# A mixture-of-experts kernel on one core: the last block of tokens merged on chip, and its output loads issued one scatter earlier

## What is computed

```python
# top-1 of 4 groups, then top-2 of 8 experts in it: 2 of 32 experts per token
combine = jnp.sum(one_hot(expert_idx, 32) * p_exp[..., None], axis=1)
for e in range(32):
    hid = silu(t @ w_gate[e]) * (t @ w_up[e])        # 1024 -> 256
    out = out + combine[:, e:e + 1] * (hid @ w_down[e])
x = x + out
y = x * rsqrt(mean(x * x) + 1e-6) * g_final
```

## Time and profile before

| what | value |
|---|---|
| time, median of 3 runs | 535.07 us (533.61 to 535.42) |
| the profiled execution, its own time | 534.76 us |
| its span | 532.9 us |
| granted TensorE clock, mean | 0.972 of full speed |
| PE busy in the span | 480.9 us (90%) |
| DVE busy | 237.9 us (45%) |
| ACT busy | 100.4 us (19%) |
| POOL busy | 201.0 us (38%) |
| DMA, mean over the span | 265 GB/s |

### The profile page before, as it was taken

How to read it: one execution, slowest core, us unless ns; L and a number is a source line. 1 busy time by engine, 2 the same in 40 slices (tenths; PEclk the granted TensorE clock), 3 DMA queues, 4 the chain that set the end, 5 groups by cost and what they waited for, 6 DMA issues and landing times.

```text
span 532.9 us, 8838 instructions
## 1 busy us (share of the span) xinstructions
PE 480.9 (90%) x3269; PEld 282.0 (53%) x3270; DVE 237.9 (45%) x513; ACT 100.4 (19%) x204; POOL 201.0 (38%) x283
## 2 busy tenths in 40 slices
PE   6999999999999999999689998999898882998883
PEld 3777777777777545545344444443444341444431
DVE  3309999999986422245722212222112210211246
ACT  3331011102104423323311111111111100011114
POOL 3002938938598600111143444333343422244100
PEclk9999999999999999999599999999999996999998
DMA  8995008000000598023969899999999999999577
GB/s 333 310 391 149 0 1 313 3 2 0 1 1 0 189 401 338 39 68 125 412 232 413 296 417 418 412 395 419 420 419 418 419 419 419 421 418 418 219 273 261
DMA packets 34564, 141.24 MB, mean 265 GB/s; under 512 B 10160, under 2 KB 10176, under 8 KB 22249
## 3 DMA queue, kind: packets, MB, share of 16 engines
q1 hardware_dynamic: 28250, 127.91, 61.0%
q0 software_dynamic: 4960, 9.45, 4.8%
q10 hardware_dynamic: 1327, 3.49, 1.8%
HBM read 134.47 MB, written 13.17 MB: 277 GB/s over the span
## 4 chain that ended last, share of the span: by engine, by line
PE 67%; DMA 14%; issue 6%; SPq 4%; DVE 4%; ACT 3%; POOL 1%; DVEq 0%; POOLq 0%; ACTq 0%
PE bank L1289 25%; PE bank L1375 10%; PE bank L1493 7%; PE bank L1513 7%; PE bank L1488 6%; DMA z<-in_w_up 6%; DMA region_x<-in_w_up 6%; PE bank L1296 5%; SPq L412 2%; DMA slot<-y_rows 2%; PE bank L1253 1%; PE bank L1503 1%; PE bank L1441 1%; DVE ua L1183 1%; DVE ua L1185 1%
## 5 line engine op out<-in xcount | busy, mean ns | idle before, releaser
L1289 PE MATMUL bank<-region_h,region_w 128*128 128x256 f32 (+1 forms) x544 | 132.7, 406 | 0.0
L1289 PEld LDWEIGHTS bank<-region_h,region_w 128*128 128x128 f32 x544 | 103.2, 190 | 28.2
L1183 DVE TENSOR_TENSOR ua<-ua,bank 128x128 f32<-128x128 f32 x30 | 8.6, 288 | 171.8 <-ACT ua L648 171.8
L1375 PE MATMUL bank<-region_w,z 128*128 128x512 f32 x128 | 56.7, 596 | 0.2 <-ACT z L593 0.2
L1513 PE MATMUL bank<-region_w,ua 128*32 128x512 f32 x328 | 49.9, 598 | 3.2 <-DVE ua L1185 3.1
L732 POOL TENSOR_TENSOR ub<-region_x 128x512 f32<-128x512 f32 x4 | 31.4, 7840 | 54.9 <-ACT region_x L536 54.9
L942 DVE SCALAR_TENSOR_TENSOR z<-ub,par,z 128x512 f32<-128x512 f32 x60 | 47.6, 794 | 0.0
L805 POOL COPY gcol<-gidx 128x1 uint32 (+1 forms) x30 | 5.4, 179 | 106.5 <-DVE sb_rows L1172 104.0
L942 DVE SCALAR_TENSOR_TENSOR region_x<-ub,par,region_x 128x512 f32<-128x512 f32 x56 | 45.5, 813 | 0.0
L1493 PE MATMUL bank<-region_w,z 128*32 128x256 f32 x512 | 44.3, 400 | 0.0
L1375 PEld LDWEIGHTS bank<-region_w,z 128*128 128x128 f32 x128 | 23.8, 190 | 28.0 <-issue 26.3
(11 more groups left out here) (250 smaller groups left out, 684.0 us busy)
## 6 DMA issues: line engine op xcount, KB each, us to landing
region_w<-in_w_down SPq DMA_DIRECT2D x21, 1024.0 KB, 13.8
region_w<-in_w_gate SPq DMA_DIRECT2D x16, 1024.0 KB, 13.3
region_w<-in_w_up SPq DMA_DIRECT2D x16, 1024.0 KB, 15.3
region_w<-in_w_in SPq DMA_DIRECT2D x3, 2048.0 KB, 21.5
slot<-in_w_gate SPq DMA_DIRECT2D x6, 1024.0 KB, 14.4
slot<-in_w_up SPq DMA_DIRECT2D x6, 1024.0 KB
slot<-in_w_down SPq DMA_DIRECT2D x6, 1024.0 KB, 13.8
region_x<-in_w_up SPq DMA_DIRECT2D x5, 1024.0 KB
```

Of the source, the lines that this page charges most:

```text
L1183: nc.vector.tensor_tensor(hid, sg_m, ps[1][:, P:2 * P], ALU.mult).then_inc(s_hid, 1)
L1289: ins = mm(ps[2 * bank + j][:, 0:LEN[j]], sec[name][:, k, c * P:(c + 1) * P], hT[:, k, CUT[j]], start=(k == 0), stop=(k == KC - 1))
L1375: ins = mm(ps[2 * (t % 2) + j][0:n, :], z[:, k, t * P:t * P + n], w_out_sb[:, k, j * 512:(j + 1) * 512], start=(k == order[0]), stop=(k == ...
```

## The change

The last block is no longer scattered and read back.

- **Table.** From the routing one-hots (`ohr`: for each token and choice the row of its block) ACT and DVE build, before block 0, a matrix `sel_in`: for each token and each row of a block, the routing weight if the token lies in the last block at that row, else 0. PE transposes it in five pieces, ACT copies it to `sel` (64 rows of the block, twice, by 576 tokens).
- **Last block.** ACT copies it from PSUM to `ylast` in SBUF. In `last_block` PE multiplies `sel` by it into the PSUM banks of a tile. Rows 0 to 63 of `ylast` hold the left 512 columns of the output, rows 64 to 127 the right 512, and each goes with its own half of `sel`'s rows to its own bank.
- **Zeros.** Before the loop POOL scatters zeros to the last block's rows of y_rows.
- **Loads.** SP waits for the zeros and for all scatters but that of the last block, then loads. The two pieces of the samples come in one transfer of 512 KB on 128 partitions. The pieces go to the places of weight slots 2 and 3 in place of 0 and 1.
- **End.** PE ends tiles 1 and 4, in place of 1 and 3. Tiles 0, 2 and 3 are DVE's: `merge` adds the last block's part from PSUM, and for tile 3 PE also puts the residual there, which DVE takes up in `add_last`. The small sum of the variance term is ACT's, in place of POOL's.
- **Residual.** The products of identity and x1 for tiles 1 and 4 stand before the last pair of experts; the 32 idle products are gone.

The diff, cut to its core:

```diff
 
-BY_PE = (1, 3)
+SAMPLES = NT - 1
+
+IN_PSUM, BY_DVE = (1, 4), (0, 2, 3)
+
+FINAL = {0: (1, 2), 1: (4, 5), 2: (3, 0), 3: (1, 2), 4: (6, 7)}
 
...
 
-        yg = [[(SLOT0 if k == 0 else RW)[:, t * D:(t + 1) * D] for t in range(NT)] for k in range(2)]
+        yg = [[RW[:, lo + t * D:lo + (t + 1) * D] for t in range(NT)] for lo in (0, 2 * SEC + 3 * PART)]
+
...
+        sel_in = ua_t[:, 3 * P + D:3 * P + D + NT * P].rearrange("p (t r) -> p t r", t=NT)
+        sel = ua_t[:, 3 * P + D:3 * P + D + NTOK]
+        nothing = ub_t[:, 0:D // 2]
+        ylast = RX[:, 0:D // 2]
 
         ident = sb("ident", [P, P])
...
+            odd1 = sp.value_load(bound[0:1, ODD1:ODD1 + 1], min_val=0, max_val=1)
+            sp.wait_ge(s_clear, 16)
...
+
+            def load_y(t):
+                for k in range(2):
+                    sp.dma_start(yg[k][t], y_dram[k * NTOK + t * P:k * NTOK + (t + 1) * P, :]).then_inc(s_yg[k][t], 16)
+
+            for t in (0, 2, 1):
+                load_y(t)
...
+
+            sp.dma_start(yg[0][SAMPLES], y_dram.rearrange("(k r) d -> k r d", k=2)[:, SEQ:NTOK, :]).then_inc(s_ygs, 16)
+            load_y(3)
...
+            act.wait_ge(s_w2, 1)
+            act.dma_start(w2s[T:P, :], w12[0:T, NT + SAMPLES:NT + SAMPLES + 1]).then_inc(s_w2s, 16)
+            act.wait_ge(s_inv, 1)
+            act.wait_ge(s_wlast, 1)
+            for t in range(NT):
+                nc.scalar.activation(sel_in[:, t, :], ohr[:, 2 * t + 1, :], ACT.Copy,
+                                     scale=wlast[:, 2 * t + 1:2 * t + 2]).then_inc(s_selk, 1)
+            act.wait_ge(s_selT, 1)
+            nc.scalar.activation(sel[:, 0:4 * P], ps[6][:, :], ACT.Copy)
+            nc.scalar.activation(sel[:, 4 * P:NTOK], ps[7][:, 0:NTOK - 4 * P], ACT.Copy).then_inc(s_sel, 1)
...
@@ -653,11 +695,15 @@
 
             for b in range(2):
                 block_of(0, b)
-            with act.Fori(1, pairs) as q:
+            with act.Fori(1, pairs1) as q:
                 for b in range(2):
                     block_of(q, b)
-            with act.If(odd > 0):
-                block_of(pairs, 0)
+            with act.If(odd1 > 0):
+                block_of(pairs1, 0)
+
+            gated(total)
+            act.wait_ge(s_down, total)
+            nc.scalar.activation(ylast, ps[3][:, :], ACT.Copy).then_inc(s_ylast, 1)
...
+            pool.tensor_copy(slast[:, 0:1], sidx[:, bass.ds(total - 1, 1)]).then_inc(s_sl, 1)
...
+            pool.wait_ge(s_sl, 1)
+            pool.tensor_tensor(carry[:, 3:4], carry[:, 1:2], carry[:, 1:2], ALU.add)
+            pool.indirect_dma_start(y_half, bass.IndirectOffsetOnAxis(ap=slast[:, 0:1], axis=0), nothing, None,
+                                    bounds_check=4 * NTOK - 1, oob_is_err=False).then_inc(s_clear, 16)
+            with pool.Fori(0, pairs1) as h:
...
+            with pool.If(odd1 > 0):
+                scatter(pairs1 * 2, 0, pairs1 * 2 + 2)
...
+            link(nc.vector.tensor_tensor(inlast, inlast, unrow, ALU.mult))
+            dve.wait_ge(s_w2, 1)
+            nc.vector.tensor_tensor(wlast.rearrange("p (t k) -> p k t", k=2), inlast.rearrange("p (t k) -> p k t", k=2),
+                                    w12.rearrange("p (k t) -> p k t", k=2), ALU.mult).then_inc(s_wlast, 1)
+            dve.wait_ge(s_wlast, 1)
+            for t in range(NT):
+
+                dve.wait_ge(s_selk, t + 1)
+                nc.vector.scalar_tensor_tensor(out=sel_in[:, t, :], in0=ohr[:, 2 * t, :], scalar=wlast[:, 2 * t:2 * t + 1],
+                                               in1=sel_in[:, t, :], op0=ALU.mult, op1=ALU.add).then_inc(s_selin, 1)
 
 
             dve.wait_ge(s_tab, 1)
...
+            dve.wait_ge(s_w2s, 16)
+            nc.vector.tensor_scalar(diag_samples[T:P, :], ident[T:P, T:P], w2s[T:P, :], None, ALU.mult).then_inc(s_diag, 1)
...
+            def merge(t):
+
+                at = BY_DVE.index(t)
+                dve.wait_ge(s_sum, at + 1)
+                dve.wait_ge(s_lastin, at + 1)
+                for j in range(2):
+                    xh = x1[:, t, j * 512:(j + 1) * 512]
+                    ins = nc.vector.tensor_tensor(xh, xh, ps[FINAL[t][j]][:, :], ALU.add)
+                ins.then_inc(s_fin, 1)
+
+            def add_last(t):
+
+                dve.wait_ge(s_yg[0][t], 16)
+                dve.wait_ge(s_lastin, BY_DVE.index(t) + 1)
+                for j in range(2):
+                    ins = nc.vector.scalar_tensor_tensor(out=x1[:, t, j * 512:(j + 1) * 512],
+                                                         in0=yg[0][t][:, j * 512:(j + 1) * 512], scalar=w12[:, t:t + 1],
+                                                         in1=ps[FINAL[t][j]][:, :], op0=ALU.mult, op1=ALU.add)
+                ins.then_inc(s_fin1, 1)
+
+            def add_end(t):
+                dve.wait_ge(s_yg[1][t], 16)
+                dve.wait_ge(s_fin1, len(BY_DVE))
+                nc.vector.scalar_tensor_tensor(out=x1[:, t, :], in0=yg[1][t], scalar=w12[:, NT + t:NT + t + 1],
+                                               in1=x1[:, t, :], op0=ALU.mult, op1=ALU.add).then_inc(s_fin, 1)
...
             add_row(0, 0)
             add_row(0, 1)
+            merge(0)
             add_row(2, 0)
+            add_row(2, 1)
+            merge(2)
             normed(0)
-            add_row(2, 1)
-            add_row(4, 0)
+            add_last(3)
             normed(2)
-            add_row(4, 1)
-            for t in (1, 4, 3):
-                normed(t)
+            normed(1)
+            add_end(3)
+            normed(4)
+            normed(3)
...
+            for t in range(NT):
+                n = TROWS[t]
+                pe.wait_ge(s_selin, t + 1)
+                ins = tr(ps[6 + t // 4][:, (t % 4) * P:(t % 4) * P + n], sel_in[0:n, t, :], ident[0:n, 0:n])
+            ins.then_inc(s_selT, 1)
...
+            def residual(t):
+                n = TROWS[t]
+                for j in range(2):
+                    ins = mm(ps[FINAL[t][j]][0:n, :], ident[0:n, 0:n], x1[0:n, t, j * 512:(j + 1) * 512], start=True, stop=False)
+                return ins
+
+            pe.wait_ge(s_sel, 1)
+            for t in IN_PSUM:
+                residual(t)
             for i in range(0, NE % NSLOT, 2):
                 pair_of(NE // NSLOT, i)
...
-            pe.wait_ge(s_diag, 2 * len(BY_PE))
-            for i, t in enumerate(BY_PE):
+            def last_block(t, first=False):
+                n = TROWS[t]
+                for h in range(2):
+                    ins = mm(ps[FINAL[t][h]][0:n, :], sel[h * T:(h + 1) * T, t * P:t * P + n], ylast[h * T:(h + 1) * T, :],
+                             start=first, stop=t in BY_DVE)
+                return ins
+
+            pe.wait_ge(s_ylast, 1)
+            last_block(0, True).then_inc(s_lastin, 1)
+            pe.wait_ge(s_diag, 4)
+            last_block(2, True).then_inc(s_lastin, 1)
+            for t in IN_PSUM:
+                last_block(t)
+            pe.wait_ge(s_fin, 1)
+            residual(3)
+            last_block(3).then_inc(s_lastin, 1)
+            t = IN_PSUM[0]
+            for k in range(2):
+                pe.wait_ge(s_yg[k][t], 16)
                 for j in range(2):
-                    mm(ps[4 + 2 * i + j][:, :], ident[:, :], x1[:, t, j * 512:(j + 1) * 512], start=True, stop=False)
-            keep_busy(32, 1)
-            for i, t in enumerate(BY_PE):
-                for k in range(2):
-                    pe.wait_ge(s_yg[k][t], 16)
-                    for j in range(2):
-                        ins = mm(ps[4 + 2 * i + j][:, :], diag[i][k], yg[k][t][:, j * 512:(j + 1) * 512],
-                                 start=False, stop=(k == 1))
-                ins.then_inc(s_comb, 1)
+                    ins = mm(ps[FINAL[t][j]][:, :], diag[k], yg[k][t][:, j * 512:(j + 1) * 512], start=False, stop=(k == 1))
+            ins.then_inc(s_comb, 1)
+            pe.wait_ge(s_ygs, 16)
+            for j in range(2):
+                ins = mm(ps[FINAL[SAMPLES][j]][0:T, :], diag_samples, yg[0][SAMPLES][:, j * 512:(j + 1) * 512], start=False, stop=True)
+            ins.then_inc(s_comb, 1)
```

More of the change, by code:

```diff
@@ L144, in build_step @@
         st_p = pst
-        diag = [[pst[:, (2 * i + k) * P:(2 * i + k + 1) * P] for k in range(2)] for i in range(len(BY_PE))]
+        diag = [pst[:, k * P:(k + 1) * P] for k in range(2)]
+        diag_samples = pst[:, 2 * P:2 * P + NS * SL]
         hist_t = sb("hist_b", [P, D])
@@ L271, in build_step @@
         s_wexp = [[sem(f"s_wexp{i}_{n}") for n in ("gate", "up", "down")] for i in range(NSLOT)]
-        s_yg = [[sem(f"s_yg{k}_{t}") for t in range(NT)] for k in range(2)]
+        s_yg = [[sem(f"s_yg{k}_{t}") for t in range(SAMPLES)] for k in range(2)]
+        s_ygs = sem("s_ygs")
         s_sq3 = sem("s_sq3")
@@ L676, in _ @@
                     act.wait_ge(s_sq3, at + 1)
                     act.wait_ge(s_eps3, i + 1)
-                    nc.scalar.activation(small[:, 40 + t:41 + t], small[:, 16 + t:17 + t], ACT.Sqrt,
```

(33 more changed lines are left out.)

103 lines of the change are left out of this document (57 added, 46 removed).

## The result

| what | value |
|---|---|
| time after, median of 6 runs | 539.68 us (537.98 to 542.26) |
| time before, beside it, median of 6 runs | 535.25 us (532.92 to 537.41) |
| ratio, with its 95% interval | 1.0087 [1.005, 1.0125] |
| the profiled execution, its own time and its span | 540.12 us, 538.6 us |
| granted TensorE clock, mean | 0.966 |

What follows compares the result with a forecast made beforehand. Bounds: weights until 482.6 us, PE until 504.7, then the last block's scatter and y_rows loads. With loads early, block 29 3.2 us late and new PE and DVE lists, DVE ends 3.0 us earlier: 535.07 to 532.1 us, range 530.8 to 536.0.

Steps and rivals of the forecast that it cites:

- Part 1: Loads of y_rows at the end: first issue at 501.3 us instead of 508.54, all landing early enough, by 517.0 us.
- this sign: Sign in the new profile that the prediction is wrong: DVE waits for a load.
- What costs nothing: Ahead of block 0: table building and five transposes fit idle gaps; if the transposes overran, up to 0.3 us lost.
- Part 2: Block 29: residual products of tiles 1 and 4 now ahead of it delay it by 3.2 us (3.1 to 3.7).
- Part 3: PE's list after the last block: each pair of 64-row products costs 0.86 us; PE ends tile 1's products at 518.3.
- Pairs in turn: Rival, PE's last-block pairs: row groups take turns, 0.86 us more per pair, 4.3 in all, time 536.4; chance 0.13.
- Part 4: DVE's list at the end, with merges and add_last: starts adding at 507.4 us, last norm ends at 526.4.
- The sum: Whole kernel: DVE ends at 526.4 against 529.38, 3.0 us less; median from 535.07 to 532.1 us, -0.56%.

Runs made afterwards that it cites:

- the one with 19 warming products: Kernel before plus five unused transposes ahead of block 0, with 19 instead of 24 useless products that keep PE busy there: ratio 0.9982.
- the pair of runs: The change again, and the change with 19 instead of 24 useless PE products ahead of block 0: 1.0071 and 1.0043 of the kernel before.
- the pair of runs on the kernel before: Kernel before plus five transposes, with 24 and with 19 useless PE products ahead of block 0: ratios 1.0048 and 0.9982.

## Why the prediction was wrong

**Part 1 failed, in "so the loads leave the chain".** The first half of it held: the first load is issued 4.41 us after the copy of block 28, against 501.3 - 497.12 = 4.18, and no load is late for the first add. What failed is how the landing of the others was found. The prediction took 10.3 and 15.7 us from the first issue out of the trace of before, as if the ten transfers were the same. They aren't: the samples' two became one of another form, and it stands ahead of tile 3. It went by the size (512 KB, the same) and not by the outermost dimension. The first piece of tile 3 landed 526.6 - 504.06 = 22.5 us after the first issue. The narrow form costs 5.9 us of the tail. The prediction named this sign (if DVE waits for a load), but no rival had the mechanism, which is why the range missed too.

**"What costs nothing" failed as well, by a way that it did not look at.** In their place the transposes did cost nothing: they fit the gap. But they moved all later instructions of PE, and 40 us on a stall came that wasn't there. That was 2.6 us more than before in the run with the transposes alone, and 3.5 us between that run and the one with 19 warming products (1.0048 less 0.9982, each against its own runs of before); in the change itself about 1.5 us (1.0071 less 1.0043), with intervals that overlap.

**Part 2 held.** 3.2 us were forecast; block 29's silu came 4.31 us after block 28's copy before and 7.45 us after, 3.14 more. Taking it back gained nothing while loads were late (38.6 us of tail, and 33.5 against 33.2 with two transfers).

**Part 3 held.** Five pairs at 0.86 us forecast, measured 3.85 / 4 = 0.96, with the joint behind it. *Pairs in turn* is out (1.46 us was the price from which it decides). Tile 1's products took 3.70 us as forecast.

**Part 4 held, once the loads are wide.** From its first add to its last norm DVE was to take 19.0 us; in the run with two transfers it takes from 506.53 to 524.86 + 1.28 = 526.14, or 19.6 us, of which it waits 1.4 for a load.

**The sum.** 3.0 us less was forecast. The tail of the version with two transfers is 2.6 to 2.9 us shorter than that of before, and with PE's stream as before its ratio of 0.9933 holds the forecast of 532.1 / 535.07 = 0.9944 in its interval. The change loses 5.9 us by the transfer, which is measured, and about 1.5 by the stream, which the pair of runs doesn't decide; with the 3.0 us of the forecast these make up the 4.4 us.

**Still open.** What PE waits for in the stall. The list of queues on the page of after has one for instructions (packets, MB, share):

```profile
q8 instruction: 20, 0.33, 0.2%
```

That is 20 packets of 0.33 / 20 MB, about 16 KB each. The Trainium skill (Runtime: NRT & Kernel Launch, "Instruction fetch mechanics") has instructions arrive in blocks of 16 KiB through a queue of the engine's own, and says that crossing into a new block is mostly hidden. The size agrees. That the stall depends on the place in the stream is shown by the pair of runs on the kernel before. The traces' DMA records bear on what arrives there: in every one of the 14 profiles a packet of 16384 bytes on q8 ends near the middle of block 5, in after at 311.19 us, 1.31 us before PE goes on. In the twelve profiles that have the pause, of 0.36 to 1.33 us, PE goes on 1.25 to 1.53 us after that packet's end, though the pause itself begins anywhere from 0 to 1.1 us after it. So the pauses fit a wait for such a block. It isn't shown: most of these packets have no pause behind them, as the next in after, which ends at 318.52 us. Open too is why the stall is 1.33 us and followed by the clock of 0.50 in two profiles, and 0.5 to 1.2 us without it in the six others with 24 warming products and the five transposes.

## What to carry to other kernels

When two transfers become one, read the outermost dimension of the new one before its bytes: at two, 512 KB ran at the share of two engines of sixteen and held up the full-width transfer behind it, and two plain transfers were 5.9 us faster. A term taken from the trace of before holds only for a transfer or product of the same form. Instructions that fit a gap aren't yet free: they shift the list of their engine, so look for stalls without a releaser far behind the edit, and try the edit with the count of instructions ahead kept as it was.

## What the runs showed of the hardware

- In block 5 a packet of 16384 bytes on the instruction queue took 0.94 to 0.98 us, and where PE paused there it went on 1.25 to 1.53 us after the end of that packet (twelve profiles).
- A transfer of 512 KB whose outermost dimension was 2 kept the DMA engines at a share of 0.12 to 0.13 and 49 to 53 GB/s, where full transfers ran at 1.04 and 401 GB/s in the same tail.
- Two products over 64 rows each, on different halves of the array and into different banks, took 0.96 us per pair; a full product of 512 columns took 3.70 / 4 = 0.93 by the same reckoning.
- Ten instructions more on PE (five products with their weights) ahead of a hardware loop brought a stall of 1.33 us some 40 us later, with the granted clock at 0.50 behind it; with ten fewer ahead of them the pause there was 0.36 us and the clock stayed at 1.00.
- The same four records of the samples' products took 1.93 us at full clock in the run with two transfers, but 3.60 us in after, where PE had been idle for 3.83 us and the clock was 0.50 (526 to 527 us).
